# Dilated keys held once with the logarithm of their count in the bias, and two steps of the sample batch moved forward

## What is computed

```
DIL_CONFIGS = ((128, 1), (512, 4), (2048, 16))
def _dilated_sample(q, kv_all, n_buf, slopes):
    for win, dil in DIL_CONFIGS:
        j = jnp.arange(win // dil + 1)
        idx = n_buf + jnp.arange(Tn)[:, None] - j[None] * dil
        g = kv_all[:, jnp.maximum(idx, 0)]
        s = jnp.einsum('bqhd,bqjhd->bhqj', q, g[:, :, :, 0]) * SCALE
        s = s - slopes[:, None, None] * (j * dil)
        p, lse = _masked_softmax(s, idx >= 0)
        outs.append(jnp.einsum('bhqj,bqjhd->bqhd', p, g[:, :, :, 1]))
        lses.append(jnp.transpose(lse, (0, 2, 1)))
    return _combine_dilations(outs, lses)     # weights = softmax over the three lse
```

## Time and profile before

| | |
|---|---|
| time, median of 3 runs | 2346.24 us (2341.94 to 2347.63) |
| span of the profiled execution | 2350.6 us |
| TensorE matmul busy | 2262.0 us, 96% |
| TensorE weight loads busy | 1618.1 us, 69% |
| VectorE, GpSimd, ScalarE busy | 891.3 us, 647.0 us, 566.5 us |
| DMA | 448.21 MB, 191 GB/s on average |

### The profile page before, as it was taken

How to read it: one execution, slowest core, us unless ns; L and a number is a source line. 1 busy time by engine, 2 the same in 40 slices (tenths; PEclk the granted TensorE clock), 3 DMA queues, 4 the chain that set the end, 5 groups by cost and what they waited for, 6 DMA issues and landing times.

```text
span 2350.6 us, 43764 instructions
## 1 busy us (share of the span) xinstructions
PE 2262.0 (96%) x13712; PEld 1618.1 (69%) x13712; DVE 891.3 (38%) x2374; ACT 566.5 (24%) x1356; POOL 647.0 (28%) x719
## 2 busy tenths in 40 slices
PE   7999999999999999999999999999999999999998
PEld 4545567676766777777745556667676677777776
DVE  2003764333353222336510147434344522233374
ACT  2111651112122422220111046311111133221202
POOL 0001760101043343344100047410102424343340
PEclk8999999999999999999999999999999999999999
DMA  9643017888864454455375320387888535444441
GB/s 348 218 165 94 6 55 269 294 295 288 301 251 149 167 185 167 167 194 193 115 268 197 134 63 0 133 301 283 306 286 299 211 117 205 179 180 172 167 167 41
DMA packets 128819, 448.21 MB, mean 191 GB/s; under 512 B 17953, under 2 KB 89890, under 8 KB 107554
## 3 DMA queue, kind: packets, MB, share of 16 engines
q1 hardware_dynamic: 118768, 416.45, 48.6%
q10 hardware_dynamic: 9906, 29.98, 3.7%
HBM read 435.76 MB, written 152.57 MB: 250 GB/s over the span
## 4 chain that ended last, share of the span: by engine, by line
PE 89%; issue 4%; DVE 4%; DMA 1%; POOL 1%; ACT 1%; DVEq 0%; SPq 0%; POOLq 0%; ACTq 0%
PE bank L1067 39%; PE bank L1150 14%; PE bank L1363 10%; PE bank L1431 3%; PE bank L1539 3%; PE bank L1298 2%; PE bank L1330 2%; PE bank L1310 2%; PE bank L1163 1%; PE bank L1485 1%; PE bank L1564 1%; POOL zone L919 1%; PE bank L1048 1%; PE bank L1511 1%; PE bank L1541 1%
## 5 line engine op out<-in xcount | busy, mean ns | idle before, releaser
L1067 PE MATMUL bank<-zone,ring 128*128 128x288 f32 x1664 | 426.3, 408 | 9.2 <-DVE zone L1704 6.6
L1067 PEld LDWEIGHTS bank<-zone,ring 128*128 128x128 f32 x1664 | 316.1, 191 | 103.0 <-DVE zone L1704 12.0
L1067 PE MATMUL bank<-zone,w 128*128 128x288 f32 x1408 | 353.5, 406 | 0.0
L1150 PE MATMUL bank<-ring,hT 128*128 128x512 f32 (+2 forms) x800 | 334.5, 572 | 6.8 <-DMA ring<-in_w_in 5.0
L1067 PEld LDWEIGHTS bank<-zone,w 128*128 128x128 f32 x1408 | 267.5, 190 | 73.9
L1150 PEld LDWEIGHTS bank<-ring,hT 128*128 128x128 f32 (+1 forms) x800 | 149.0, 191 | 161.4 <-issue 150.2
L873 POOL TENSOR_TENSOR w<-ring 128x512 f32<-128x512 f32 x72 | 95.6, 1328 | 555.9 <-PE bank L1067 309.4
L1363 PE MATMUL bank<-ring,w 128*128 128x128 f32 x2048 | 242.5, 277 | 0.0
L1363 PEld LDWEIGHTS bank<-ring,w 128*128 128x128 f32 x2048 | 233.0, 192 | 4.1 <-issue 3.8
L611 ACT COPY zone<-bank 128x288 f32<-128x288 f32 x72 | 28.6, 398 | 569.5 <-PE bank L1067 569.5
L986 POOL TENSOR_TENSOR zone<-constants,stat 128x1024 f32<-128x1024 f32 x16 | 30.3, 1896 | 457.2 <-DVE stat L2063 457.2
(11 more groups left out here) (256 smaller groups left out, 2791.2 us busy)
## 6 DMA issues: line engine op xcount, KB each, us to landing
out_dil_s<-in_state_kv_dil SPq DMA_DIRECT2D x48, 2720.0 KB, 12.1
ring<-in_w_units SPq DMA_DIRECT2D x72, 1024.0 KB, 4.8
zone<-in_dilated_v SPq DMA_DIRECT2D x16, 3072.0 KB, 12.7
ring<-in_cache_kv_cmp SPq DMA_DIRECT2D x256, 128.0 KB, 2.2
ring<-in_cache_kv_sel SPq DMA_DIRECT2D x256, 128.0 KB, 6.1
ring<-in_w_in SPq DMA_DIRECT2D x10, 2048.0 KB, 8.6
zone<-in_dilated_k SPq DMA_DIRECT2D x16, 1280.0 KB, 6.0
zone<-in_dilated_k SPq DMA_DIRECT2D x16, 1024.0 KB, 8.1
```

The source lines that it names most:

```text
L1067: last = mm(dst[:, 0:HALF], lhs[:, k, :], rhs(k), start=first and k == 0, stop=(k == 3), skip_group_check=True)
L1150: last = mm(dst, hT[:, k, t * P:t * P + ROWS[t]], ring[:, n % 2, k * CH:k * CH + width], start=start and k == 0, stop=stop and k == KT - 1)
```

## The change

A key of the dilated mixer that two or three of the (window, dilation) sets share was held, scored and multiplied once for each; now it is held once. The last 128 past keys stay one tile. The step-4 class keeps 96 past keys a tile, and the batch's own eight new keys stand behind them in each of the four tiles (104 keys). The two step-16 classes keep 96 keys a tile. The bias `b_dil` holds minus slope times distance plus the log of how many sets hold the key, over 128 + 104 + 96 = 328 columns, where there were 384 + 64. So the extra score matmuls over new keys (L1465), the extra value product over new keys (L1541), VectorE's second pass with its minimum, and the fourth transpose go away. The new keys are copied into the tiles by GpSimd (`new_keys`), and TensorE's batch waits for that copy instead of for the load; the new values come by a DMA from the output that the layer has already written. The values now take four loads a batch (`vd_ld` counts four), and 96 of 128 partitions for twelve of the thirteen tiles. ScalarE copies the three transposes one by one, and the value products wait for each.

Two things are only moved. The compressed values (before L1491) and ScalarE's copy of them stand ahead of the importance. On VectorE the group sums come ahead of the new-score pass of the selected branch.

```
-CH_L, CH_A, CH_S = 6, ROUNDS * 4, 13
+NEAR, FAR = 96, 96
+K_NEAR = NEAR + NS
+AT_NEAR, AT_FAR = P, P + K_NEAR
+KEYS_D = AT_FAR + FAR
+KA, KB = 4 * P + 16 * K_NEAR, 16 * FAR
+CH_L, CH_A, CH_S = 6, ROUNDS * 4, 11
...
+    nn = ((dd >= 0) & (dd <= 128)).astype(int) + ((dd >= 0) & (dd <= 512) & (dd % 4 == 0)) + ((dd >= 0) & (dd % 16 == 0))
+    nn[:, AT_FAR:] *= ~void
+    c["b_dil"] = np.where(nn > 0, -sd * dd + np.log(np.maximum(nn, 1)), NEG).astype(f)
...  (sync queue)
-                    sp.dma_start(vd[:, a:z, :], of_batch("dilated_v", b)[:, a:z, :]).then_inc(vd_ld.sem, 16)
+                def load_dilated_v(b):
+                    sp.dma_start(vd[:, 0, :], i["dilated_v_last"][L, ds(b, 1)].rearrange("o q p f -> (o q p) f")).then_inc(
+                        vd_ld.sem, 16)
+                    sp.dma_start(vd[0:NEAR, 1:ND_TILES - 1, :], of_batch("dilated_v", b)[:, 0:ND_TILES - 2, :]).then_inc(
+                        vd_ld.sem, 16)
+                    new = o["dil_s"][L, ds(b, 1), PAST - NS:PAST, CH:2 * CH].rearrange("o q r f -> (o q r) f")
+                    sp.dma_start(vd[NEAR:K_NEAR, 1:5, :], new.unsqueeze(1).to_broadcast([NS, 4, CH])).then_inc(vd_ld.sem, 16)
+                def load_last_v(b):
+                    sp.dma_start(vd[0:NEAR, ND_TILES - 1:ND_TILES, :], of_batch("dilated_v", b)[:, ND_TILES - 2:ND_TILES - 1, :]).then_inc(
+                        vd_ld.sem, 16)
...  (scalar)
+                    act.wait_ge(sc_full.sem, sc_full.at(it, SC_VC + 1))
+                    copy(vc, bank[SC_BANK[SC_VC]][:, 0:P]).then_inc(kv_act.sem, 1)
                     act.wait_ge(td_full.sem, td_full.at(it, TD_PTC + 1))
...
-                    copy(ptd[:, 0:3, :].rearrange("p e r -> p (e r)"), B[:, 0:384])
-                    copy(ptd[0:64, 3, :], B[0:64, 384:512]).then_inc(ptk_act.sem, 1)
+                    for e, R in enumerate((P, K_NEAR, FAR)):
+                        copy(ptd[0:R, e, :], B[0:R, e * P:(e + 1) * P]).then_inc(ptk_act.sem, 1)
...  (gpsimd)
+                def new_keys(it, b):
+                    pool.wait_ge(s_pad.sem, s_pad.at(it, 1))
+                    pool.wait_ge(kda_ld.sem, kda_ld.at(it, 1))
+                    nc.gpsimd.tensor_copy(kd_near[:, :, :, NEAR:K_NEAR],
+                                          knb[:, :, ds(b * NS, NS)].unsqueeze(1).to_broadcast([P, 4, 4, NS])).then_inc(
+                                              kd_new.sem, 1)
...  (tensor)
-                    pe.wait_ge(kda_ld.sem, kda_ld.at(it, 1))
+                    pe.wait_ge(kd_new.sem, kd_new.at(it, 1))
...
-                    for p in range(4):
-                        mm(S[:, 384:448], strips[:, 0, p * P:(p + 1) * P], knb[:, p, :], start=False, stop=(p == 3),
-                           skip_group_check=True)
...
-                    mm(bank[7][:], ptd[0:64, 3, :], vsm[:, 256:768], start=False, stop=True,
-                       skip_group_check=True).then_inc(od_full.sem, 1)
...  (vector)
-                    negated(s_d[:, 0:384], B[:, 0:384], const["b_dil"][:], sm[:, 24:25])
-                    step(new_scores(s_d[:, 384:448], B[:, 384:448], const["nb_newd"][:, new], sm[:, 25:26]))
-                    V.tensor_reduce(stat[:, 26:27], sm[:, 24:26], X, ALU.min).then_inc(td_used.sem, 1)
+                    negated(s_d, B[:, 0:KEYS_D], const["b_dil"][:], stat[:, 26:27]).then_inc(td_used.sem, 1)
```

More of the change, by code:

```diff
@@ L890, in _ @@
                     kind, t = z_kind(n)
-                    if kind not in ("cs", "wg", "vb"):
+                    if kind not in ("cs", "wg", "vb") or n == NZ - 1:
                         continue
@@ L994, in _ @@
                 pad(l * NB)
+                new_keys(l * NB, 0)
                 with pool.Fori(0, NB - 1) as b:
@@ L1471, in batch @@
                         sc_full.sem, 1)
+                    B = bank[SC_BANK[SC_VC]]
+                    for k in range(2):
+                        last = mm(B[:, k * HD:(k + 1) * HD], hid[:, 1, k * P:(k + 1) * P], w2[:, 1, :],
+                                  start=(k == 0), stop=(k == 1), skip_group_check=True)
+                    last.then_inc(sc_full.sem, 1)
                     pe.wait_ge(s_gs.sem, s_gs.at(it, 1))
@@ L1488, in batch @@
                         last.then_inc(sc_full.sem, 1)
-                    B = bank[SC_BANK[SC_VC]]
-                    for k in range(2):
-                        last = mm(B[:, k * HD:(k + 1) * HD], hid[:, 1, k * P:(k + 1) * P], w2[:, 1, :],
-                                  start=(k == 0), stop=(k == 1), skip_group_check=True)
-                    last.then_inc(sc_full.sem, 1)
                     pe.wait_ge(kda_ld.sem, kda_ld.at(it, 2))
@@ L2206, in laid_out, with turned @@
     put["state_kv_dil"] = dil.reshape(DEPTH, NB, PAST, D)
-    by4 = dil[:, :, PAST - 4 * P:].reshape(DEPTH, NB, P, 4, 2, 8, HD)
-    by16 = dil.reshape(DEPTH, NB, P, 16, 2, 8, HD)[:, :, :, 0:8]
-    tiles = np.concatenate([dil[:, :, PAST - P:, None], by4, by16], 3)
-    put["dilated_v"] = tiles[..., 1, :, :].reshape(DEPTH, NB, P, ND_TILES, CH)
-    put["dilated_k"] = tiles[..., 0, :, :].reshape(DEPTH, NB, P, ND_TILES, 4, 2, HD).transpose(
-        0, 1, 5, 6, 3, 4, 2).reshape(DEPTH, NB, P, ND_TILES, CH)
+    last = dil[:, :, PAST - P:]
+    near = dil[:, :, PAST - WIN:PAST - P].reshape(DEPTH, NB, NEAR, 4, 2, 8, HD)
+    far = dil.reshape(DEPTH, NB, P, 16, 2, 8, HD)[:, :, 0:FAR, 0:8]
+    put["dilated_v_last"] = last[..., 1, :, :].reshape(DEPTH, NB, P, CH)
+    put["dilated_v"] = np.concatenate([near, far], 3)[..., 1, :, :].reshape(DEPTH, NB, NEAR, ND_TILES - 1, CH)
+    def turned(rows, room):
+        k = rows[..., 0, :, :].reshape(DEPTH, NB, rows.shape[2], -1, 4, 2, HD).transpose(0, 1, 5, 6, 3, 4, 2)
+        k = np.pad(k, [(0, 0)] * 6 + [(0, room - rows.shape[2])])
+        return k.reshape(DEPTH, NB, P, -1)
+    put["dilated_k"] = np.concatenate([turned(last[:, :, :, None], P), turned(near, K_NEAR), turned(far, FAR)], -1)
     return {n: np.ascontiguousarray(v) for n, v in put.items()}
```

94 lines of the change are left out of this document (46 added, 48 removed).

## The result

The kernel became slower. Before it takes 2346.1 us and after 2372.3 us (medians of four runs each, 2365.2 to 2378.4 after); the ratio is 1.0113, 95% interval 1.0088 to 1.0137. Forecast were 2305 us and a range of 2290 to 2321.

The account below looks back on a forecast made before the run. TensorE's work and the gaps in its chain were taken to bound each batch; 1.02 + 0.52 + 1.00 + 0.15 - 0.10 = 2.59 us a batch, x16 = 41.4 us, gave 2305 us, range 2290 to 2321.

Parts of the forecast that it names:

- term E: Raw pages for the next batch's compression: queue times stay, cover shrinks, a slow page costs a little; -0.10 us a batch.
- What rides along: GpSimd's new-key copy, shorter constants and one value copy fewer: net about nothing, within 1 us.
- rival 2: Raw pages become the bound and SyncE's queue round sets the batch period: 2319 us, chance 0.15.
- rival 4: SyncE's queue sets the round because the two added value-load issues are costly (4 us each): 2375 us, chance 0.04.
- A: Batch start: four matmuls removed, group sums earlier, compressed values hidden in the importance wait; 1.02 us a batch.
- D: Dilated key classes of 104, 96 and 96 columns: between 0 and 0.69 us a batch, taken as 0.15.
- B: Dilated transposes: three instead of four, and first value tile waits only for the first copy; 0.52 us a batch.
- C: Extra value product over new keys (L1541) removed, selected exponential just covered; 1.00 us a batch.
- rival 1: Narrower keys pay in full, 0.69 us a batch, 2299 us; sign a class at 0.8 us; chance 0.17.
- cover of 1.1 us: Predicted margin between the last raw page's landing and TensorE's need for it, shrunk from 3.7 us.

Follow-up runs that it names:

- e7: Kernel before the change, with both value loads cut to 96 of 128 partitions (rows 96 to 127 not loaded): 2383.47 us, ratio 1.0150.
- e8: Changed kernel with its 96-row load of eleven value tiles cut in two, rows 0 to 63 and 64 to 95: 2381.06 us, ratio 1.0141.
- e11: Changed kernel with value tiles on 128 rows and new values loaded by ScalarE, which also issues six of sixteen selected pages: 2297.61 us, ratio 0.9799.
- e12: Kernel before the change, with three of every four score products of the narrow dilated groups reading 96 of 128 keys: 2339.85 us, ratio 0.9983.
- e5: Changed kernel with all thirteen value tiles on 128 partitions and new values loaded from ScalarE's queue, same result as the reference: 2315.59 us, ratio 0.9872.
- e1: Changed kernel with value source rows padded in DRAM to lie 26,624 bytes apart, still 96 partitions: 2371.07 us, ratio 1.0117.
- e6: As e5, but ScalarE instead of SyncE also issues the next batch's window and value loads: 2320.42 us, ratio 0.9892.

## Why the prediction was wrong

**The step that failed** is the one on the raw pages and the queue (term E, with "What rides along"). It said that the queue's times "don't move", that rival 2 had "fewer bytes on the DMA engines" against it, and of rival 4 that "an issue costs 0.46 to 0.6 us whatever its size here". The value loads were counted by bytes. The rows could not show the price of a load over 96 partitions, since every value load of the kernel before spans 128; I gave this unknown no bounds at all. Alone, such a load goes at 0.5 to 0.65 of the rate (after, e7, e8), it keeps the DMA engines busy longer, and the selected pages' issues behind it stall. The round had 6.0 us of slack; TensorE's gain of 3.2 us a batch, 4.6 us more of selected issues and the two added issues use that up. The loop then closes through the queue, the landing of the last raw page and TensorE's products, and that sets the period.

**Rival 4** named the right place and side, with a chance of 0.04, but not the mechanism; that its 2375 us lies 3 us from the result is luck. It asked for two added issues of over 5.9 us together. The four value issues cost 0.32 to 0.95 us each. It is the selected pages' issues, not changed at all, that grew. Its sum also set the queue's 33.3 us against the old period of 39.24. Beside the forecast period, 36.65, only 3.3 us were free, and 1.2 of them were spent on the added issues. Its sign, a queue without waits, came by half: the wait for the dilated output is gone (33.4 us before), and of the 50.2 us for the selected output 33.3 are left. What no rival had: behind a wait of over 3 us the products run at a granted clock near 0.50, and since the selected pages wait for those products, the loop grows by that too.

**Terms of TensorE.** They stand in a batch without a page wait (the timeline of after from 488.72 on, and of before from 443.79 on, both above; e11's stretches agree within 0.01).

| term | predicted | measured | from |
|---|---|---|---|
| A, start of the batch | 1.02 | 1.06 | first class to third: 9.07 before, 7.64 after, less D's 0.37 |
| B, transposes and first values | 0.52 | 0.48 | third class to values: 5.36, 4.67, less D's 0.21 |
| C, product over new values | 1.00 | 1.06 | values to next transposes: 5.21, 4.15 |
| D, narrower keys | 0.15 | 0.58 | 0.16 + 2 x 0.21 |

Together 3.18; e11's period is 39.24 - 36.08 = 3.16 us shorter. A, B and C were right in mechanism and size: the importance has its gap of 0.19 us, the values 0.45, and the transposes of the selected scores wait for nothing.

**D was mis-sized.** Rival 1 was nearer: 0.58 of its 0.69 us, and a class of 96 columns takes 0.80 us in the chain for 1.01, its sign. I had taken the row of L1465 as the nearest, where half the columns gave nothing; but its weights are 128 wide, and their loads (191 ns each) can cover a narrower product; that is an argument, no run changed it. With weights of 32 columns a narrower product paid (e12 too).

The rule of the Trainium skill, "TensorE: Matmul & The Clock Gate", section on LDWEIGHTS, agrees with the difference of the two rows (82 ns, 80 by the rule), but not with either of them (109 and 191 ns, 27 and 107 by the rule). My estimate from it had the eight loads of a group, one after another, at 213 ns as a floor. After, a group takes 0.80/4 = 0.20 us, 13 ns less. So the loads are not such a floor. That they overlap fits, where 96 loads of 109 ns make 2.4 us of busy time. The chance for rival 1 should have been the larger.

**Term E and rival 2**, once the rows are 128: e5 keeps 14.6 us of raw-page waits, about 1 us a round where 0.10 was forecast. The cover of 1.1 us was indeed the weak spot, and rival 2's 2319 us is close to e5's 2316. That it is so close is in part luck: with D at 0.58 its sum would have been 2312.

## What to carry to other kernels

A load that is made smaller by covering 96 partitions instead of 128 can take longer: compare GB/s of the load by itself, and pad to 128 partitions until a run says otherwise. Where a change shortens the engine that bounds, add up the loop of the queue that feeds it (issues, register reads, landing, the product that frees the buffer) and compare it with the new period, not the old one. Issues can be given to an engine that waits anyway, as ScalarE here.

## What the runs showed of the hardware

- A load over 96 partitions of 22,528 to 24,576 bytes each goes at 215 to 242 GB/s, over 128 at 381 to 418, and splitting it into 64 and 32 partitions gives 206. Why is open: source pitch is ruled out (e1), and so are idle DMA engines (107.7% of their time in after). Ports and which rows an engine gets were not told apart, and no other number of partitions was run.
- Reading sixteen page numbers on SyncE costs 11.2 to 11.4 us, 0.70 each, more than issuing the pages (8.83).
- After a TensorE wait of 2.48 us the clock stayed at 1.00, after 3.73 us the next 6.4 us of work ran near 0.50. In the kernel after, a wait of 1.11 us was followed by slow products too, and in e5 one of 1.30 but not one of 1.87, so the length of the wait alone doesn't decide.
- The longest issue of a selected page takes 3.4 us before, 4.9 in e5, 5.9 after and 8.3 in e7; a round's sixteen take 10.2, 11.4, 14.8 and 15.2 us. So they grow with the packet time of the value loads ahead of them, and they stay when ScalarE issues those loads (e6). What in the queue is full then is not shown.
